# Four output units taken tile by tile in a state space mixer, and two weight splits moved behind the first piece of a layer norm

## What is computed

```python
h = layer_norm(DN_ALPHA * h + 0.5 * swiglu(h, ffn_w1[i, 0], ffn_w3[i, 0], ffn_w2[i, 0]), ...)
if i % 2 == 0:
    hc, gb, gc, u = split(h @ ab_w_in[j])
    ya = short_conv_mixer(hc, gb, gc, conv_w[j])      # 512 columns
    yb = s5_mixer(u, ...)                             # 512 columns: out = z * sigmoid(z @ w_glu + b_glu)
    mix = concatenate([ya, yb]) @ ab_w_out[j]
else:
    mix = dsa_mixer(h @ c_w_in[j], ...) @ c_w_out[j]
h = layer_norm(DN_ALPHA * h + mix, ...)
h = layer_norm(DN_ALPHA * h + 0.5 * swiglu(h, ffn_w1[i, 1], ffn_w3[i, 1], ffn_w2[i, 1]), ...)
h = h + (p[i] @ ple_w_proj[i]) * sigmoid(h @ ple_w_gate[i])
```

## Time and profile before

| | us |
|---|---|
| median of 3 runs | 2272.46 |
| the runs | 2272.46, 2272.72, 2270.16 |
| the profiled execution | 2270.52 |
| its span, first to last instruction | 2268.7 |
| PE busy | 2206.5 (97%) |
| DVE busy | 1429.5 (63%) |
| ACT busy | 1125.6 (50%) |
| mean granted TensorE clock | 0.996 |

### The profile page before, as it was taken

The page is one execution under the profiler, slowest core; times in us unless marked ns, Lnnn a source line. Parts: engine busy times, 40 slices in busy tenths (PEclk is TensorE's granted clock), DMA queues, the critical chain, the costliest instruction groups (busy, mean ns, idle before and its releaser), DMA issues.

```text
span 2268.7 us, 25958 instructions
## 1 busy us (share of the span) xinstructions
PE 2206.5 (97%) x10482; PEld 1819.4 (80%) x10482; DVE 1429.5 (63%) x1922; ACT 1125.6 (50%) x1678; POOL 188.8 (8%) x219
## 2 busy tenths in 40 slices
PE   8999999999999999999999999979999999999999
PEld 6888878888888887778888887757888888887887
DVE  6655665655565567656555875886557555676556
ACT  6545565545454456655444453434444444464443
POOL 0000000000000020000000980540000000110000
PEclk9999999999999999999999999999999999999999
DMA  8556534565565563236666565425565656535553
GB/s 289 187 186 216 159 112 157 169 186 184 183 223 186 176 202 109 90 120 209 185 187 205 186 184 169 160 73 183 185 190 187 198 186 189 182 110 188 186 189 125
DMA packets 111144, 396.55 MB, mean 175 GB/s; under 512 B 13232, under 2 KB 14000, under 8 KB 110896
## 3 DMA queue, kind: packets, MB, share of 16 engines
q1 hardware_dynamic: 111024, 394.90, 54.5%
HBM read 393.80 MB, written 1.05 MB: 174 GB/s over the span
## 4 chain that ended last, share of the span: by engine, by line
PE 84%; DVE 11%; ACT 4%; issue 1%; DMA 1%; POOL 0%; SPq 0%; DVEq 0%; ACTq 0%; POOLq 0%
PE bank L567 26%; PE bank L569 26%; PE bank L568 25%; DVE wlo L1734 3%; PE bank L615 2%; PE bank L626 2%; PE bank L682 1%; ACT whi L1151 1%; PE bank L668 1%; DVE ab_B L2323 0%; DVE bank L2319 0%; DVE bank L2316 0%; PE bank L657 0%; DVE together L1870 0%; DVE X L1900 0%
## 5 line engine op out<-in xcount | busy, mean ns | idle before, releaser
L1734 DVE TENSOR_TENSOR wlo<-raw,whi 128x1024 fp32r<-128x1024 f32 (+2 forms) x718 | 877.8, 1260 | 227.8 <-ACT whi L1151 226.6
L1151 ACT ACTIVATE whi<-raw 128x1024 fp32r<-128x1024 f32 (+2 forms) x718 | 721.5, 1049 | 178.7 <-DMA raw<-in_w_w 89.8
L567 PE MATMUL bank<-whi,XH 128*128 128x512 f32 (+3 forms) x1840 | 725.6, 394 | 8.5 <-DVE wlo L1734 3.0
L569 PE MATMUL bank<-whi,XL 128*128 128x512 f32 (+3 forms) x1840 | 712.8, 387 | 0.0
L568 PE MATMUL bank<-wlo,XH 128*128 128x512 f32 (+3 forms) x1840 | 711.8, 387 | 0.0
L567 PEld LDWEIGHTS bank<-whi,XH 128*128 128x128 f32 x1840 | 346.4, 188 | 79.8 <-issue 8.1
L569 PEld LDWEIGHTS bank<-whi,XL 128*128 128x128 f32 x1840 | 346.2, 188 | 71.3
L568 PEld LDWEIGHTS bank<-wlo,XH 128*128 128x128 f32 x1840 | 346.9, 189 | 65.5
L567 PE MATMUL bank<-whi,HH 128*128 128x512 f32 x704 | 276.3, 392 | 0.0
L569 PE MATMUL bank<-whi,HL 128*128 128x512 f32 x704 | 274.7, 390 | 0.0
L568 PE MATMUL bank<-wlo,HH 128*128 128x512 f32 x704 | 274.5, 390 | 0.0
(11 more groups left out here) (405 smaller groups left out, 2028.2 us busy)
## 6 DMA issues: line engine op xcount, KB each, us to landing
raw<-in_w_w SPq DMA_DIRECT2D x264, 512.0 KB, 3.5
raw<-in_w_gu_pre SPq DMA_DIRECT2D x88, 512.0 KB, 3.6
raw<-in_w_gu_post SPq DMA_DIRECT2D x88, 512.0 KB, 3.6
raw<-in_w_dn_pre SPq DMA_DIRECT2D x44, 512.0 KB, 3.5
raw<-in_w_dn_post SPq DMA_DIRECT2D x44, 512.0 KB, 3.5
raw<-in_w_x_kv SPq DMA_DIRECT2D x32, 512.0 KB, 4.1
raw<-in_w_sbg_in SPq DMA_DIRECT2D x20, 512.0 KB, 4.2
raw<-in_w_x_q SPq DMA_DIRECT2D x16, 512.0 KB, 4.4
```

The source lines that it names most:

```text
L567: pe.e.matmul(o, xh, hi[:, k, :], start=kt == 0, stop=False)
L569: m = pe.e.matmul(o, xl, hi[:, k, :], start=False, stop=kt == kts - 1)
L1151: act.e.activation(whi[v % SLOTS][:, 0:n], raw[v % SLOTS][:, 0:n], ACT.Copy).then_inc(*hi_ok.did(v))
L1734: dve.e.tensor_tensor(wlo[v % SLOTS][:, 0:n], raw[v % SLOTS][:, 0:n], whi[v % SLOTS][:, 0:n].bitcast(F32), ALU.subtract).then_inc(*lo_ok.d ...
```

## The change

It has three parts. At the five layer norms that go by `schedule`, only two of the next four units are split before tile 0's last group, and the other two after "one 0" (a table `BEHIND`, and a second "split" that asks for all four). At the state space mixer's end, units 2, 3, 6 and 7 are multiplied for tile 0 and then for tile 1; all five splits that stood around the mixing now stand ahead of it, and DVE mixes c = 0 and c = 1 of tile 0, then those of tile 1. In `AB_END` a new step "ahead" asks ACT and DVE for the three splits of "half 5" before "outputs 3", and "low 3" comes before "half 5". On PE "ahead" and "low" are no work, so there the order of `AB_END` stays.

```diff
--- before.py
+++ after.py
@@ -69,6 +69,10 @@
             out.append((c, k, min(n, kts - k), w, col))
         col += w
     return out
+
+
+
+BEHIND = {"w2_0_0": 2, "w2_0_1": 2, "w2_1_0": 2, "w2_1_1": 2, "c_out": 2}
 
 
 def schedule(name, tail=False, hold=False, late=1):
@@ -105,7 +109,7 @@
             for i, k0, nk in rest:
                 yield "split", i, 0
             if last:
-                yield "split", rest[-1][0], GROUP
+                yield "split", rest[-1][0], GROUP - BEHIND.get(name, 0)
             for j, (i, k0, nk) in enumerate(rest):
                 if first and j == len(rest) - 1:
                     yield "one", 1
@@ -119,6 +123,7 @@
             for j, (i, k0, nk) in enumerate(rest):
                 if last and j == len(rest) - 1:
                     yield "one", 0
+                    yield "split", rest[-1][0], GROUP
                 yield "unit", c, i, k0, nk, 1
                 if not last:
                     yield "split", i, GROUP
@@ -142,7 +147,7 @@
             12: [("state", 6)], 13: [("outputs", 0), ("state", 7)], 14: [("low", 0)], 15: [("state", 8)]}
 AB_END = [("state", 9), ("conv", 0), ("state", 10), ("rest", 0), ("conv", 1), ("outputs", 1), ("state", 11), ("rest", 1),
           ("half", 0), ("low", 1), ("state", 12), ("half", 1), ("state", 13), ("state", 14), ("half", 4), ("outputs", 2),
-          ("state", 15), ("low", 2), ("glu", (0, 1, 2)), ("outputs", 3), ("half", 5), ("low", 3), ("glu", (3,))]
+          ("state", 15), ("low", 2), ("glu", (0, 1, 2)), ("ahead", 3), ("outputs", 3), ("low", 3), ("half", 5), ("glu", (3,))]
 
 
 class PutOff:
@@ -1010,22 +1015,20 @@
             for m in range(2):
                 held[13 + m].open_after = [(act_ok, ("glu", 2 * m + 1))]
             banks.spare = [4, 5, 6, 7]
-            half(2)
-            half(3)
-            for t in range(2):
-                ob[0][t].open_after = [(dve_ok, ("acc", "ln01", 0, t))]
-            banks.close(ob[0])
-            for i in (6, 7):
+            for i in (2, 3, 6, 7):
                 pe_split("ab_out", i, 0)
             for t in range(2):
-                for i in (6, 7):
-                    pe_unit("ab_out", 1, i, us[i][1], us[i][2], t, lhs, ob[1])
+                for i in (2, 3, 6, 7):
+                    c, k0, nk, w, _ = us[i]
+                    pe_unit("ab_out", c, i, k0, nk, t, lhs, ob[c])
                 if t == 1:
                     for x in pe_later.take((None, 0)):
                         pe_turn(x)
-                ob[1][t].open_after = [(dve_ok, ("acc", "ln01", 1, t))]
+                for c in range(2):
+                    ob[c][t].open_after = [(dve_ok, ("acc", "ln01", c, t))]
                 pe_later.add(pieces_ln("ln01")(1, (t,)))
-            banks.close(ob[1])
+            for bs in ob:
+                banks.close(bs)
 
         def pe_ds_tiles(key, src, dst, t, g, n, done):
             b = banks.scratch(("dst", key, t, g))
@@ -1543,6 +1546,9 @@
                         act_warm(ACT.Sigmoid)
                 elif what == "half":
                     half(n)
+                elif what == "ahead":
+                    act_settle()
+                    act_split_to(index["ab_out", 5] + n)
                 elif what == "glu":
                     act_settle()
                     act_split_to(index["glu", n[-1] // 2])
@@ -1567,9 +1573,6 @@
                 act.wait_ge(dve_ok, ("abglu", x))
                 act.e.activation(XH[:, 4 + 2 * x:6 + 2 * x, :], B_[:, x, :, :], ACT.Copy).then_inc(*act_ok.did(("abgh", x)))
             act_warm(ACT.Sqrt)
-            half(2)
-            half(3)
-            act_settle()
             act_split_to(index["ab_out", 7] + GROUP)
             for t in range(2):
                 if t == 1:
@@ -2359,6 +2362,9 @@
                         *dve_ok.did(("abya", 2 * n), ("abya", 2 * n + 1)))
                 elif what == "half":
                     half(n)
+                elif what == "ahead":
+                    dve_settle()
+                    dve_split_to(index["ab_out", 5] + n)
                 elif what == "glu":
                     dve_settle()
                     dve_split_to(index["glu", n[-1] // 2])
@@ -2376,16 +2382,13 @@
                 dve.wait_ge(act_ok, ("abgh", x))
                 dve.e.tensor_tensor(XL[:, 4 + 2 * x:6 + 2 * x, :], B_[:, x, :, :], XH[:, 4 + 2 * x:6 + 2 * x, :].bitcast(F32),
                                     ALU.subtract).then_inc(*dve_ok.did(("abyb", 2 * x), ("abyb", 2 * x + 1)))
-            half(2)
-            half(3)
             mixed = dve_mixed("ab_out", "ln01", 1.0)
-            mixed(0, (0, 1))
-            dve_settle()
             dve_split_to(index["ab_out", 7] + GROUP)
             for t in range(2):
                 if t == 1:
                     for x in dve_later.take((None, 0)):
                         dve_turn(x)
+                mixed(0, (t,))
                 mixed(1, (t,))
                 dve_later.add(dve_pieces_ln("ln01")(1, (t,)))
```

## The result

| | before | after |
|---|---|---|
| median, us | 2271.86 (20 runs) | 2276.48 (20 runs) |
| lowest to highest | 2267.99 to 2273.99 | 2273.09 to 2284.91 |
| ratio after / before | | 1.0024 [1.0018, 1.0031] |
| the profiled execution | 2270.52 | 2276.43 |
| its span | 2268.7 | 2274.7 |

The change costs 4.6 us by the medians and 6.0 us between the two profiled spans.

What follows compares the result with a forecast made beforehand. TensorE, busy 2206.5 of 2268.7 us, was taken as the bound, so only its idle time could be won. +5.38 - 0.53 - 0.52 = +4.33, with clock +7.7, from 2271.5 gave 2279.2 us; range 2270 to 2283.

Steps and rivals of the forecast that it cites:

- the clock's +3.4: Behind the five tails' longer second waits: PE's clock falls in two of five, +3.4 us; bounds none and five (+8.5).
- The rival without falls of the clock: Five tails: delays as replayed but PE's clock never falls behind the second waits; 2275.8 us, chance 0.24.
- T+5.11: Tail of w2_1_0: tile 1's mixing starts 5.11 us after T, the start of the first piece's transposes; before T+3.68.
- +5.38: Five tails: sum of later second waits, 1.43 us per tail, less first waits won in w2_0_0 and c_out.
- which this wait swallows: Five tails: PE needs piece 2's low half only at T+4.9 to 5; its lateness vanishes in the second wait.
- The term was 0.53 of gain: Mixer's end, units tile by tile: PE starts tile 1's first piece at 1546.62 instead of 1547.15, gain 0.53 us.
- the slow clock would stay between the pieces and hide in this wait: Mixer's end: PE's slow clock, 1.7 us lost before, now hides behind the wait for tile 1's first piece.
- 0.52: State outputs, splits ahead: PE's 1.40 us wait goes, POOL's last step is held 0.88 us; gain 0.52 us.
- The rival in which it did: State outputs: DVE keeps POOL out for all three splits, +2.5 us, 2281.7 us; chance 0.07.
- Not slower: Five tails: two splits cost tile 1 nothing, so 1.63 and 1.05 us are won; 2268.8 us, chance 0.14.
- not moved: Five tails: the change doesn't move the splits, a later request finds them done; 2270.4 us, chance 0.05.
- faster: Tails cost nothing and the mixer's end also gives back its 3.05 and 1.7 us; about 2264 us, chance 0.05.

Runs made afterwards that it cites:

- part1_only: Kernel before with only the tail change: two of four splits behind the first piece in five tails; 2276.32 us, ratio 1.0023.
- mix_first: parts2_3_only, but in the five tails DVE mixes tile 1 before subtracting tile 0's piece 2 (its low half); 2264.37 us, ratio 0.9971.
- pe_kept_busy: Changed kernel with 16 extra identity transposes on PE before tile 1's first piece at all six norms; 2274.07 us, ratio 1.0009.
- parts2_3_only: Changed kernel with `BEHIND` empty, so all four splits stand ahead in the five tails as before; 2270.28 us, ratio 0.9992.
- part2_only: Kernel before with only the mixer's last four units done tile by tile, `AB_END` as before; 2271.58 us, ratio 1.0001.
- three_behind: Changed kernel with three splits instead of two behind the first piece in the five tails; 2283.71 us, ratio 1.0056.
- mix_first_mixer_too: mix_first, and at the mixer DVE mixes tile 1's first column half between the low halves of tile 0's two pieces; 2262.9 us, ratio 0.9957.

## Why the prediction came out right, and where it did not

- **The number.** The forecast was 2279.2 us and +7.7; the median is 2276.48 and +4.6, inside the range, and the ratio's interval (4.1 to 7.0 us) leaves out 7.7. The term that was too large is the clock's +3.4. The rival without falls of the clock gave 2275.8 and lies nearer, although the falls that it leaves out are there in the trace. So the sign and the delay come from the mechanism, and the nearness of 4.6 to 4.33 is in part luck.
- **Part 1.** Right in mechanism and size. Mixing at T+5.10 for a forecast T+5.11, and +5.21 in the trace for a forecast +5.38. part1_only shows that it carries the loss, and the series of one, two and three splits that the cause is the length of the splits beyond DVE's idle 1.12. The 1.63 of first waits was won, but over traces of the same tails that figure runs from 0.91 to 2.37.
- **The second waits** were forecast as 2.1, 1.9, 2.4, 2.4 and 2.0 and are 2.08, 1.60, 2.05, 2.04 and 1.62. The step that failed is "which this wait swallows": piece 2's low half is late too, and PE waits for it just before (in w2_1_0 0.34 of the 1.41 falls there). The sum is the same, but the idle time is in two bits.
- **Part 2.** The term was 0.53 of gain up to tile 1's first piece. It measured 0.62: from the first of the four units' matmuls to that piece 22.07 us before and 21.45 after; DVE's last step of the norm came no later, where the text had 0.10. The first wait fell to 1.69 (forecast 1.9). (One step of 1.33 brings DVE from 1533.3 to 1534.6; the text says two, but counts one.) But the wait at tile 1's piece is 2.10, where the text said 0.6 or more. The step that failed is that the slow clock would stay between the pieces and hide in this wait. It had followed the wait of 3.05; in this trace it didn't come there, PE was early at the piece, waited 2.10, and the slow clock came behind it, on the path, for 1.65. It can fall as the text had it: in the trace of mix_first, with the same mixer, it came at 1538.3, behind a first wait of 1.72, and the second wait was 0.50, with no slow clock behind it. mix_first's PE timeline at the mixer:

```profile
1535.74 0.66 PE L621 MATMUL bank<-together,X 128*128 128x128 f32 x4 [1.72 <-DVE X L1908]
...
1544.29 0.66 PE L621 MATMUL bank<-together,X 128*128 128x128 f32 x4 [0.50 <-DVE X L1908]
```

- **Part 3.** POOL's last step took 2.13 for a forecast 2.15, and at full clock the gain is 0.66 for 0.52. That it is 1.33 at slow clock wasn't foreseen. The Trainium skill (SBUF — State Buffer, section "SBUF: two separate sides") says that the loser of the shared port pair is fully blocked. The rows agree for single instructions (2.13 against 1.27 on POOL), and a row of several splits didn't keep POOL out beyond one of them. The rival in which it did is excluded by 2.13. The text's "2.19 against 1.27" sets two different POOL steps side by side; the like one is 2.15 against 1.27.
- **The clock.** I took two falls in five tails. The trace has two, behind w2_1_0 and c_out, and a third at the mixer. Each cost 1.58 to 1.65, for an estimate of 1.7. The trace's 6.0 for a forecast 7.7 comes out of two things that the sum didn't have: this trace lost the two slow stretches of before at 916.7 and 943.98 (-3.16), and it has the mixer's on the path (+1.65). The medians differ by 4.6, near the 4.33 of the sum without the clock; pe_kept_busy says that the clock has a share in this nevertheless. Slow stretches at 919 and 947 us are in the trace of part1_only too and not in that of parts2_3_only, though the code up to there is the same, so a count of falls in one trace is no measure of the mean. Two falls in five was a guess from a few waits, and its agreement with this one trace is luck: part1_only has none in five. How the medians' 4.6 divides between delay and clock stays open beyond that.
- **Rivals.** "Not slower" is excluded by T+5.10, "not moved" by the two splits between the pieces. The "faster" one named a mechanism that is real, but the order of after hasn't got it: mix_first reached 2264.37 by filling the same idle time with the mixing.

## What to carry to other kernels

An idle gap in a queue is worth only its own length: one split of 1.15 us went into 1.12 us of idle time nearly free, each further one delayed what was behind it by 1.13. Fill a gap first with the step that the next wait hangs on, not with work that has no hurry: with the mixing in the gap, at the mixer too, the time was 0.9957 of before, where parts 2 and 3 alone gave 0.9992. Read the second wait before moving work to shorten the first. And compare two traces stretch by stretch: slow clock in places that the change doesn't touch moved this one by 3.16 us.

## What was not expected of the hardware

- Slow clock came behind PE waits of 2.04, 2.05 and 2.10, and did not behind 2.08 (w2_0_0) in the same trace. Over all twelve traces PE waited 2.03 to 2.10 us at a piece 15 times; slow clock followed 8 times. Behind 2.33, ahead of the mixer's last four units, it came in five traces of twelve (part1_only, part2_only, part3_only, three_behind and mix_first_mixer_too). The length of one wait in this zone doesn't decide it.
- Behind six waits that were filled with 1.91 us of transposes the granted clock was 1.00. This is one trace; part1_only's had 1.00 behind its five second waits without them.
- A slow clock can hide another cost: with it, PE waited 0.41 us for POOL instead of 1.65.
- A chain on another engine can hide the slow clock. With the mixer's new order the stretch up to tile 1's first piece is 21.43 to 21.45 us in the seven traces where DVE mixes in the changed kernel's order there, with slow clock in it (part2_only, three_behind, mix_first) or not.
